# The gate product in two passes, the first unit's products between the transposes of x, the second unit's weight parts ahead of the gate rows

## What is computed

```
proj = x @ w_in                       # 1024 -> 2568 columns
u_pool, q, k, v, o_pre, gates = split(proj)      # 512 | 512 | 512 | 512 | 512 | 8
gates = gates + b_gate;  ig, fg = gates[:4], gates[4:]
y_pool = pooling mixer of u_pool (windows 2, 4, 8, 16)
h      = mLSTM(q, k, v, ig, fg)       # 4 heads of 128, running max, chunks
mix    = concat(y_pool, sigmoid(o_pre) * h) @ w_out
x1     = layernorm(alpha * x + mix)
y      = layernorm(alpha * x1 + relu(x1 @ w_ff1 + b)**2 @ w_ff2 + b)
```

## Time and profile before

| | us |
|---|---|
| median of 3 executions | 1173.37 |
| lowest, highest | 1171.72, 1175.47 |
| the profiled execution, its own time | 1174.68 |
| its span in the trace | 1173.0 |
| PE busy | 1132.3 (97%) |
| DVE, ACT, POOL busy | 554.7, 435.7, 90.1 |

### The profile page before, as it was taken

The page is one execution under the profiler, slowest core; times in us unless marked ns, Lnnn a source line. Parts: engine busy times, 40 slices in busy tenths (PEclk is TensorE's granted clock), DMA queues, the critical chain, the costliest instruction groups (busy, mean ns, idle before and its releaser), DMA issues. The chain is left out here.

```text
span 1173.0 us, 18969 instructions
## 1 busy us (share of the span) xinstructions
PE 1132.3 (97%) x7856; PEld 1114.5 (95%) x7856; DVE 554.7 (47%) x898; ACT 435.7 (37%) x644; POOL 90.1 (8%) x110
## 2 busy tenths in 40 slices
PE   7999999999999999999999999979999999999993
PEld 5999999999888999899999999979999999999993
DVE  5612222226475755863444444345445344354367
ACT  4622424332343765745455444460202202202022
POOL 4000000010011221000000000000000000000055
PEclk9999999998999999999999999989999999999997
DMA  9221111131044542223323242480412403404012
GB/s 244 74 71 37 39 37 39 37 111 35 4 134 156 185 128 73 84 73 111 107 94 121 73 142 72 161 304 3 145 41 105 144 6 138 144 0 144 1 49 96
DMA packets 81570, 110.29 MB, mean 94 GB/s; under 512 B 4121, under 2 KB 65145, under 8 KB 81508
## 3 DMA queue, kind: packets, MB, share of 16 engines
q1 hardware_dynamic: 77964, 98.94, 25.5%
q0 software_dynamic: 3552, 10.59, 3.0%
HBM read 85.95 MB, written 23.79 MB: 94 GB/s over the span
## 5 line engine op out<-in xcount | busy, mean ns | idle before, releaser
L1396 PE MATMUL bank<-x_hi,w_hi 128*128 128x344 f32 (+1 forms) x792 | 261.8, 330 | 2.4 <-DVE x_lo L1097 1.4
L1396 PE MATMUL bank<-x_hi,w_lo 128*128 128x344 f32 (+1 forms) x792 | 254.7, 322 | 0.0
L1396 PE MATMUL bank<-x_lo,w_hi 128*128 128x344 f32 (+1 forms) x792 | 254.3, 321 | 0.0
L1396 PE MATMUL bank<-h_hi,w_hi 128*128 128x344 f32 x768 | 246.9, 321 | 7.6 <-issue 7.6
L1396 PE MATMUL bank<-h_hi,w_lo 128*128 128x344 f32 x768 | 246.4, 321 | 0.0
L1396 PE MATMUL bank<-h_lo,w_hi 128*128 128x344 f32 x768 | 246.1, 321 | 0.0
L1396 PEld LDWEIGHTS bank<-x_hi,w_hi 128*128 128x128 f32 (+1 forms) x792 | 148.8, 188 | 9.8 <-issue 3.8
L1396 PEld LDWEIGHTS bank<-h_hi,w_hi 128*128 128x128 f32 x768 | 145.5, 189 | 7.7 <-issue 7.7
L1396 PEld LDWEIGHTS bank<-x_hi,w_lo 128*128 128x128 f32 (+1 forms) x792 | 148.5, 187 | 1.1
L1396 PEld LDWEIGHTS bank<-x_lo,w_hi 128*128 128x128 f32 (+1 forms) x792 | 148.6, 188 | 1.0
L1396 PEld LDWEIGHTS bank<-h_hi,w_lo 128*128 128x128 f32 x768 | 145.3, 189 | 0.0
(11 more groups left out here) (271 smaller groups left out, 1652.0 us busy)
## 6 DMA issues: line engine op xcount, KB each, us to landing
w_raw<-in_w_ff SPq DMA_DIRECT2D x18, 1024.0 KB, 6.4
h_raw<-hidden SPq DMA_DIRECT2D x24, 688.0 KB, 9.8
hidden<-h_unit SPq DMA_DIRECT2D x28, 516.0 KB, 2.9
s_raw<-in_w_ff SPq DMA_DIRECT2D x14, 1024.0 KB, 5.8
w_raw<-in_w_out SPq DMA_DIRECT2D x12, 1024.0 KB, 5.2
w_raw<-in_w_in SPq DMA_DIRECT2D x16, 512.0 KB, 5.4
x_nat_all<-in_x_prompt SPq DMA_DIRECT2D x6, 512.0 KB, 7.7
x_nat<-in_x_prompt POOLq DMA_DIRECT2D x6, 512.0 KB, 4.0
```

The source lines that it names most:

```text
L1396: return nc.tensor.matmul(out, lhsT, rhs, start=start, stop=stop, skip_group_check=True)
```

## The change

It has five parts.

1. The low parts of the gate weights no longer lie in a tile of their own but in columns 64 to 67 and 96 to 99 beside the high ones, which are in 0 to 3 and 32 to 35 (`GATE_ROWS` is 100). A gate product is now 16 matmuls, both x parts with these 100 columns. Its low rows are copied out by ACT (`gate_lo_rows`), and DVE adds high rows, bias and low rows (`gate_rows_sum`), in place of ACT's two instructions. The gate results use bank 7 and semaphores of their own (`gate_done`, `gate_low`, `gate_sum`).
2. SP issues unit 1's weights ahead of tiles 3 to 8 of x, and ACT and DVE split them right after block 0.
3. PE's order becomes x_block(0), gates(0), product 0 of unit 1, x_block(1), product 1, x_block(2), gates(1), product 2, gates(2), the transposes of the small states, products 3 to 5. Unit 1 now goes block by block (q and k of block 0, then of block 1, then of block 2), no longer q of all blocks and then k.
4. ACT and DVE make the high and low parts of unit 2's weights before the gate rows, right after the last gate product. Unit 2 starts from `lo_done >= 3` as before.
5. On ACT only result (1,3) stands between the ln and `rows_hi`, (1,4) behind it, and (1,5) behind the three exps and the last copy. The transposes of the gate rows (`colT`) come after product 4 of unit 2, and no longer after product 1.

```diff
-GATE_ROWS = 36
+GATE_ROWS = 100
...
         @block.sync
-            for t in range(3, len(TILES)):
-                token_dma(sp, XNAT[0:TILES[t][1], t, :], a["x_prompt"], a["x_sample"], t, True, x_in[t])
             for u in range(1, U_OUT):
                 kind, j = PROJ[u - 1]
+                if u == 2:
+                    for t in range(3, len(TILES)):
+                        token_dma(sp, XNAT[0:TILES[t][1], t, :], a["x_prompt"], a["x_sample"], t, True, x_in[t])
                 if u >= 2:
                     sp.wait_ge(lo_done, u - 1)
...
         @block.scalar
-                if u >= 2:
+                if u == 2:
+                    act.wait_ge(gate_done, NBLK)
+                elif u > 2:
                     act.wait_ge(gemm_done, outputs_to(u - 2))
...
+            def gate_lo_rows(b):
+                act.wait_ge(gate_done, b + 1)
+                if b:
+                    act.wait_ge(gate_sum, 2 * b)
+                A(GL[0:NH, 0, :], N_[64:64 + NH, 0:BLK], ACT.Copy)
+                A(GL[0:NH, 1, :], N_[96:96 + NH, 0:BLK], ACT.Copy).then_inc(gate_low, 1)
...
+            for s in range(6):
+                x_hi_part(s)
+            split_hi(0)
+            split_hi(1)
+            gate_lo_rows(0)
+            evac(1, 0)
+            for s in range(6, 12):
+                x_hi_part(s)
+            evac(1, 1)
+            for s in range(12, 18):
+                x_hi_part(s)
+            gate_lo_rows(1)
+            evac(1, 2)
+            gate_lo_rows(2)
+            split_hi(2)
...
-            evac(1, 0)
-            evac(1, 1)
-            split_hi(2)
+            evac(1, 3)
             act.wait_ge(dve_row, ROW_NEGM)
             A(RBH[0:NH, pr], TN[0:NH, pr], ACT.Copy).then_inc(act_row, 1)
-            evac(1, 2)
+            evac(1, 4)
...
-                for i in range(3 if u == 1 else 0, 6):
+                for i in range(5 if u == 1 else 0, 6):
                     evac(u, i)
...
         @block.vector
+            def gate_rows_sum(b):
+                if b == 0:
+                    dve.wait_ge(bias_in, 16 * 3)
+                dve.wait_ge(gate_low, b + 1)
+                stt(TI[0:NH, blk(b)], N_[0:NH, 0:BLK], SMALL[0:NH, 0:1], GL[0:NH, 0, :], ALU.add, ALU.add).then_inc(gate_sum, 1)
+                stt(TF[0:NH, blk(b)], N_[32:32 + NH, 0:BLK], SMALL[0:NH, 1:2], GL[0:NH, 1, :], ALU.add, ALU.add)\
+                    .then_inc(gate_sum, 1)
+            for s in range(6):
+                x_lo_part(s)
+            split_lo(0)
             split_lo(1)
+            gate_rows_sum(0)
+            for s in range(6, 18):
+                x_lo_part(s)
+            gate_rows_sum(1)
+            gate_rows_sum(2)
+            split_lo(2)
...
-            split_lo(2)
...
         @block.tensor
             def gates(b):
                 pe.wait_ge(x_lo, 6 * b + 6)
-                split_product(bank[b][0:GATE_ROWS, 0:BLK], lambda k: gslot(WH)[:, k, :], lambda k: gslot(WL)[:, k, :],
-                              lambda k: XH[:, k, blk(b)], lambda k: XL[:, k, blk(b)], range(KC)).then_inc(gemm_done, 1)
+                if b:
+                    pe.wait_ge(gate_sum, 2 * b)
+                for k in range(KC):
+                    mm(N_[0:GATE_ROWS, 0:BLK], gslot(WH)[:, k, :], XH[:, k, blk(b)], k == 0, False)
+                    last = mm(N_[0:GATE_ROWS, 0:BLK], gslot(WH)[:, k, :], XL[:, k, blk(b)], False, k == KC - 1)
+                last.then_inc(gate_done, 1)
...
+            pe.sem_inc(gemm_done, N_GATE)
+            pe.sem_inc(gemm_read, N_GATE)
             x_block(0)
-            x_block(1)
             pe.wait_ge(lo_done, 1)
             gates(0)
+            pe.wait_ge(lo_done, 2)
+            first_unit(0)
+            x_block(1)
+            first_unit(1)
             x_block(2)
             gates(1)
+            first_unit(2)
             gates(2)
...
+            for i in range(3, 6):
+                first_unit(i)
...
-            for u in range(1, U_OUT):
+            for u in range(2, U_OUT):
                 pe.wait_ge(lo_done, u + 1)
...
-                    if u == 2 and i == 1:
+                    if u == 2 and i == 4:
```

More of the change, by code:

```diff
@@ L150, in build_layer @@
         assert base + cur[0] <= nc.sbuf_usable_end, (base + cur[0], nc.sbuf_usable_end)
+        GL = at("gate_lo", [P, 2, BLK], o_lay)
         VM = at("v_masked", [P, 2, 4, P], o_lay)
@@ L188, in build_layer @@
         stT_ready, stT_read = sem("stT_ready"), sem("stT_read")
+        gate_done, gate_low, gate_sum = sem("gate_done"), sem("gate_low"), sem("gate_sum")
         act_row, dve_row = sem("act_row"), sem("dve_row")
@@ L462, in keep @@
                 for j in js:
-                    pool.wait_ge(gemm_read, N_GATE + 12 * h + 3 * j + 3)
+                    pool.wait_ge(gemm_read, N_GATE + (6 if h == 0 and j == 0 else 12 * h + 3 * j + 3))
                     G.tensor_copy(SM[:, j, h, :], QKV[h % 2][:, j, sa]).then_inc(smp_kept, 1)
@@ L551, in _, with x_hi_part @@
             A(SMALL[:, 3:4], ONES[:, 0:1], ACT.Copy)
-            for s in range(2 * len(TILES)):
+            def x_hi_part(s):
                 t0, n = TILES[s // 2]
@@ L558, in _ @@
                   bank[3 + s % 4][:, :].rearrange("p (k n) -> p k n", k=4)[:, :, 0:n], ACT.Copy).then_inc(x_hi, 1)
[L559 to L572, removed]
+            def gate_lo_rows(b):
[4 more added lines that the diff above has]
+                A(GL[0:NH, 1, :], N_[96:96 + NH, 0:BLK], ACT.Copy).then_inc(gate_low, 1)
             def evac(u, i):
                 kind, j = PROJ[u - 1]
-                f, b = i // 3, i % 3
+                f, b = (i % 2, i // 2) if u == 1 else (i // 3, i % 3)
                 n = N_GATE + 6 * (u - 1) + i
@@ L589, in evac @@
                     A(Y[:, 4 + j, blk(b)], src, ACT.Sigmoid).then_inc(gemm_read, 1)
-            act.wait_ge(gemm_read, NBLK)
+            for s in range(6):
[13 more added lines that the diff above has]
+            split_hi(2)
+            act.wait_ge(stT_ready, 1)
+            A(CST[:, :], B_[:, 0:92], ACT.Copy).then_inc(stT_read, 1)
+            act.wait_ge(stT_ready, 2)
+            A(SPT[:, :, :, :].rearrange("p g b r -> p g (b r)"),
+              S_[:, :].rearrange("p (g n) -> p g n", g=4)[:, :, 0:NS * NBUF], ACT.Copy).then_inc(stT_read, 1)
+            act.wait_ge(gate_sum, 2 * NBLK)
             A(TZ[0:NH, :], TF[0:NH, :], ACT.Abs).then_inc(act_row, 1)
@@ L871, in split_lo @@
                 if u == 0:
[L872 to L874 removed]
+                    raw, hi, lo = wslot(RAW, 0), gslot(WH).bitcast(F32), gslot(WH)
+                    V.tensor_tensor(lo[:, :, 64:64 + NH], raw[:, :, 0:NH], hi[:, :, 0:NH], ALU.subtract)
+                    V.tensor_tensor(lo[:, :, 96:96 + NH], raw[:, :, NH:2 * NH], hi[:, :, 32:32 + NH],
                                     ALU.subtract).then_inc(lo_done, 1)
@@ L889, in after_rows @@
                 dve.wait_ge(dve_row, row_n[0])
-            V.memset(WL[:, 1, 0:KC * GATE_ROWS].bitcast(F32), 0.0)
             row(V.memset(WH[:, 1, 0:KC * GATE_ROWS].bitcast(F32), 0.0), ROW_PAD)
@@ L898, in _, with x_lo_part @@
             row(V.memset(RBL[:, :].bitcast(F32), 0.0), ROW_INV)
-            for s in range(2 * len(TILES)):
+            def x_lo_part(s):
                 t0, n = TILES[s // 2]
@@ L1445, in _ @@
             last.then_inc(stT_ready, 1)
-            def unit_product(u, f, b, n, ks=range(KC), before=None):
-                pe.wait_ge(gemm_read, n - 2)
-                cs = slice(P * f, P * (f + 1))
-                return split_product(bank[n % 3][:, 0:BLK], lambda k: wslot(WH, u)[:, k, cs], lambda k: wslot(WL, u)[:, k, cs],
-                                     lambda k: XH[:, k, blk(b)], lambda k: XL[:, k, blk(b)], ks, before)
+            for i in range(3, 6):
+                first_unit(i)
             def att1(p):
```

12 lines of the change are left out of this document (8 added, 4 removed).

## The result

| | us |
|---|---|
| before, median of 14 runs (lowest, highest) | 1173.37 (1170.61, 1175.47) |
| with the change, median of 14 runs (lowest, highest) | 1176.24 (1173.68, 1181.57) |
| ratio | 1.0028, 95% interval 1.0017 to 1.0039 |
| predicted | 1175.8, 1171.5 to 1179.0 |

The change costs 2.9 us, against 2.4 forecast.

The account below looks back on a forecast made before the run. PE, busy 97% of the span, was taken to bound the kernel. Head -1.7, late results +4.0 and handoffs +0.1 gave +2.4 us, on the median 1173.4 making 1175.8 us; range 1171.5 to 1179.0.

Parts of the forecast that it names:

- the first part: Up to unit 2's start: 24 gate matmuls fewer, partly lost to waits; unit 2 begins at 50.6, not 52.3, minus 1.7 us.
- the sum: Whole forecast for the change: -1.7 + 4.0 + 0.1 for handoffs = +2.4 us.
- What bounds the kernel: PE is busy 97% of the span, so only what PE issues and where it waits counts.
- the step to product 0: Head of unit 1: weights land at 12.2, splitting takes 4.24 us, PE waits 2.6 us, from 13.9 to 16.5.
- The bounds (11.0 to 14.2): Earliest and latest landing of unit 1's weights, making the head minus 2.9 or plus 0.3 us.
- gates(0): Block 0's gate product on PE: after 1.8 us idle, runs 11.4 to 13.9 at 0.157 us a matmul.
- the part on the clock: Early clock fall: slow gates(0) ends inside the wait for unit 1's weights, costing nothing; in product 0 or 1, 1.2 us.
- The second part: Unit 2: results (1,4) and (1,5) come out late; second and third products wait 1.7 and 2.3 us, plus 4.0.
- The first one: Rival: clock falls after 16.5 us in unit 1's first products, 1.2 us a spell; +3.6 us, 1177.0; chance 0.20.
- The second rival: Queue order does not decide when unit 1's weights land, 14.2 or later; +4.4 us, 1177.8; chance 0.16.
- the third: Rival: unit 1's results are not late in unit 2; only -1.7 us, 1171.7; chance 0.12.
- the fourth: Rival: the 24 gate matmuls come out whole, early landing and no late result; -3.8 us, 1169.6; chance 0.10.

Follow-up runs that it names:

- one tile ahead: The changed kernel with tile 3 of x loaded ahead of unit 1's weights; 1180.60 us, ratio 1.0064 to the kernel before.
- the halves: The changed kernel with results (1,3) to (1,5) and (2,0) taken out early and unit 1's weights split in two halves; 1170.30 us, 0.9974 to the kernel before.
- three copies moved: The changed kernel with ACT's copies of results (1,4), (1,5) and (2,0) moved earlier; 1171.97 us, ratio 0.9989 to the kernel before.
- the late split: The changed kernel with the early split of unit 2's weights alone undone on ACT and DVE; 1182.70 us, ratio 1.0076 to the kernel before.
- the first early results: The changed kernel with only results (1,4) and (1,5) taken out ahead of the wait for row_negM; 1174.19 us, ratio 1.0004 to the kernel before.
- the two passes alone: The kernel before with only gate products of 16 matmuls and low rows added by DVE, nothing reordered; 1173.97 us, ratio 1.0003.
- the third pass: The changed kernel with a zero-weight matmul added to each slice, so a gate product has 24 matmuls again; 1178.50 us, 1.0039 to the kernel before.

## Why the prediction was right

The time (1175.8 against 1176.24) and the direction came out, and the experiments say that the reasons were the right ones. Two errors offset each other in part: the first part gave 0.9 us less than forecast and the waits cost 0.3 less, so the trace has 3.0 where the sum had 2.4. The change's second measurement, 2.0, lies on the other side of the forecast.

*What bounds the kernel.* Right: the 3.0 us by which unit 2 ends later are the 2.9 of the medians, and from there to 279 us no matmul is moved any further.

*The first part, minus 1.7 us.* The right sign, half the size: 0.8. The term that was mis-sized is the step to product 0. Unit 1's weights landed at 12.96 and not at 12.2, the split took its 4.24 us as said (14.91 + 2.29 = 17.20), and product 0 began at 17.25 in place of 16.5. From there every step kept its length: 17.25 to 51.50 is 34.25 us, forecast 16.5 to 50.6, 34.1. The bounds (11.0 to 14.2) held the landing. That the landing hangs on the place in the queue was shown by the run with one tile ahead; its steepness, 3.6 us a tile, was not foreseen.

*gates(0).* Forecast 11.4 to 13.9. It began at 11.38, and its last matmul at 15.80, at half clock: 0.29 us a matmul, where the sum had 0.157. So this term was wrong by 2.1 us. The wait in front of product 0 hid all of it, as the part on the clock had said for that case, though in this trace the clock did not fall early but had no record of full clock before 17.0. The run with the halves shows that it is no longer hidden once that wait is gone.

*The second part, plus 4.0 us.* Right in each step. From E, the end of the last gate matmul (39.52 + 0.32 = 39.84): ln ends at 47.74, E + 7.9 (forecast 8.2, since ACT's copy of a low gate row takes 0.45 us and not 0.54); `row_negM` at 55.25, E + 15.4 (15.7); (1,4) out at 56.67, E + 16.8 (17.1); (1,5) at 62.80, E + 23.0 (23.2). The second product begins 1.4 us late (forecast 1.7) and the third 3.8 (4.0). The run with three copies moved took 3.3 us away, which shows the cause.

*The rivals.* The first one did happen in single traces. The clock fell at 11.4 (and again at 62.7) in the second trace of the change, at 12.1 and 56.5 with the late split, at 16.6 with the first early results, at 17.8 with one tile ahead and at 29.3 with the two passes alone. The falls at 11.4 and 12.1 ended inside the wait for unit 1's weights and cost nothing, those at 16.6 and 17.8 reached product 0 and cost 1.4 and 1.7 us, where the prediction had 1.2 a spell. It was a rival to the forecast for good reason, but in the medians the change does not pay more than the waits themselves. What I had put wrongly is the place: I looked for it in the first products of unit 1 only, and the pauses of unit 2 are as good a place. The rule of the Trainium skill (TensorE: Matmul & The Clock Gate, the section on the HAM clock gate), that the clock falls after an idle stretch, is borne out in so far as each of these falls follows a pause or lies in one; but the traces show falls without a stretch that was idle throughout, and there the measurement decides. At 62.7 the engine had been busy 1.92 of the 4.00 us before, and at 278.6 in the kernel before its one pause, in front of a matmul at 276.75, had been 1.01 us long. The second rival fell (the weights land at 12.96, inside my bounds), the third too (both results were late), and the fourth, that all 3.8 us of the matmuls come out: in the new order the third pass was worth 2.8 us at most, in the old one 1.1 at most.

## What to carry to other kernels

When work is moved ahead of a serial chain, count on the engine that runs the chain what stands behind it in the list, and compare its date with that of the first product that needs it: here two result copies of 0.43 us behind 15 us of row work cost 3.8 us of a 97% busy engine, with a third one next in line (1.33 us), and moving the three gave it back. A wait on a count of results ("all but the last two") is a wait on the whole list of the engine that makes them. And work that is taken off the critical engine in a stage where that engine waits for a load or a split gives nothing until the wait goes too; splitting the awaited operand in halves (0.9989 to 0.9974, from two sessions and with overlapping intervals) was worth about as much as the removed matmuls.

## What the runs showed of the hardware that was not expected

- The granted clock decides about single executions more than this change does. Behind unit 2, spells of 0.50 lay in the same few stages, but not in all of them each time: near 780 us in every trace (6.8 or 10.2 us long) and at the kernel's end, near 280 and 370 us (3.4 or 6.8 us) in the kernel before and not in the first profiled execution of the change, near 490 us in its second and in most variants but in neither of these two. So the profiled execution of the slower kernel was the shorter one.
- At the start the trace's first record of the full clock stands at 9.0 us before. In the two traces of the change it stood at 17.0 and at 8.0, so the date is not fixed by the kernel. In the first of these gates(0) took 0.29 us a matmul throughout (the page's PEclk shows 1.00 there, as it has no record before 17.0), and so the spacing of the matmuls has to be read and not PEclk. Matmuls of zeros that nobody reads brought the full clock to 6.2 and 5.0 us in the two traces that have them.
- SP needed 5.28 us to issue two loads of 512 KB in pieces of 512 bytes, against 3.72 us for six loads of tiles of x; the loads behind them were issued later by as much.
